# A fused decoder step on one core: 51 conditioning loads issued by ScalarE's queue instead of SyncE's

## The reference

```python
mod = (jax.nn.silu(c) @ w_ada + b_ada)[:, None, :]
sh1, sc1, gt1, sh2, sc2, gt2 = jnp.split(mod, N_MOD, axis=-1)
h = rmsnorm(x, g_pre_mix) * (1.0 + sc1) + sh1
m, k_rows, v_rows, s_new = token_mixer(h, w_in, ..., w_out, k_past, v_past, s0)
x = x + gt1 * rmsnorm(m, g_post_mix)
h = rmsnorm(x, g_pre_ffn) * (1.0 + sc2) + sh2
f = (jax.nn.silu(h @ w_ffn_gate) * (h @ w_ffn_up)) @ w_ffn_down
x = x + gt2 * rmsnorm(f, g_post_ffn)
```

## Time and profile before

| | |
|---|---|
| median of 3 runs | 1491.46 us (1487.97 to 1493.14) |
| the profiled execution | 1489.45 us, of it 1487.7 us from its first to its last instruction |
| busy, share of that span | PE 96%, PEld 85%, DVE 62%, ACT 45%, POOL 7% |
| DMA queue of SP | 319.59 MB, 63.1% of the 16 DMA engines' time |
| DMA queue of POOL | 76.10 MB, 13.5% |
| DMA queue of ACT (64 packets) | 0.07 MB, 0.0% |
| HBM traffic over the span | 265 GB/s |

### The profile page before, as it was taken

The page is one execution under the profiler, slowest core; times in us unless marked ns, Lnnn a source line. Parts: engine busy times, 40 slices in busy tenths (PEclk is TensorE's granted clock), DMA queues, the critical chain, the costliest instruction groups (busy, mean ns, idle before and its releaser), DMA issues.

```text
span 1487.7 us, 29187 instructions
## 1 busy us (share of the span) xinstructions
PE 1428.6 (96%) x11232; PEld 1270.8 (85%) x11232; DVE 922.3 (62%) x1519; ACT 665.3 (45%) x1303; POOL 105.8 (7%) x203
## 2 busy tenths in 40 slices
PE   7779999999899999999999999999999999999997
PEld 2237787887668787796999999999999999999997
DVE  2234588996778667369856766566665675446444
ACT  1023477677655554445543434334344343334333
POOL 0000311113322210000000000000000000200000
PEclk9969999999899999999999999999999999999999
DMA  9999999999999979987666666665666655855552
GB/s 368 421 341 359 388 392 406 379 345 397 392 396 336 342 258 354 404 323 278 221 181 184 178 179 179 181 185 171 183 181 174 185 173 190 233 179 181 182 177 95
DMA packets 139330, 396.82 MB, mean 267 GB/s; under 512 B 13162, under 2 KB 17681, under 8 KB 126433
## 3 DMA queue, kind: packets, MB, share of 16 engines
q1 hardware_dynamic: 117954, 319.59, 63.1%
q0 software_dynamic: 21232, 76.10, 13.5%
q10 hardware_dynamic: 64, 0.07, 0.0%
HBM read 382.28 MB, written 11.34 MB: 265 GB/s over the span
## 4 chain that ended last, share of the span: by engine, by line
PE 84%; DMA 9%; DVE 3%; ACT 2%; issue 1%; POOLq 0%; SPq 0%; POOL 0%; DVEq 0%; ACTq 0%
PE ps L1997 24%; PE ps L1998 24%; PE ps L1999 24%; PE ps L1931 4%; DMA ada_s<-in_w_ada 4%; DMA v_page<-in_cache_v 2%; PE ps L2129 2%; DMA ada_r<-in_w_ada 1%; DMA k_page<-in_cache_k 1%; PE ps L2055 1%; ACT k_page L815 1%; PE ps L1974 0%; DVE k_page L1328 0%; DVE w_lo L1277 0%; ACT w_hi L727 0%
## 5 line engine op out<-in xcount | busy, mean ns | idle before, releaser
L1997 PE MATMUL ps<-h_hi,w_hi 128*128 128x264 f32 x2304 | 666.9, 289 | 6.1 <-DVE h_lo L1265 3.6
L1998 PE MATMUL ps<-h_lo,w_hi 128*128 128x264 f32 x2304 | 658.6, 286 | 0.0
L1999 PE MATMUL ps<-h_hi,w_lo 128*128 128x264 f32 x2304 | 658.2, 286 | 0.0
L1997 PEld LDWEIGHTS ps<-h_hi,w_hi 128*128 128x128 f32 x2304 | 438.1, 190 | 49.1 <-issue 33.6
L1822 DVE TENSOR_TENSOR w_lo<-raw,w_hi 128x1024 fp32r<-128x1024 f32 x254 | 307.2, 1214 | 273.1 <-ACT w_hi L1059 271.7
L1059 ACT ACTIVATE w_hi<-raw 128x1024 fp32r<-128x1024 f32 x264 | 278.5, 1059 | 403.2 <-PE ps L1999 391.0
L1998 PEld LDWEIGHTS ps<-h_lo,w_hi 128*128 128x128 f32 x2304 | 437.4, 190 | 0.5
L1999 PEld LDWEIGHTS ps<-h_hi,w_lo 128*128 128x128 f32 x2304 | 436.3, 189 | 0.0
L1277 DVE TENSOR_TENSOR w_lo<-raw,w_hi 128x1024 fp32r<-128x1024 f32 x138 | 168.8, 1224 | 144.4 <-ACT w_hi L727 143.9
L727 ACT ACTIVATE w_hi<-raw 128x1024 fp32r<-128x1024 f32 x128 | 135.1, 1056 | 174.7 <-PE ps L1999 156.3
L1998 PE MATMUL ps<-act_lo,w_hi 128*128 (+1 forms) x704 | 200.5, 285 | 0.0
(11 more groups left out here) (363 smaller groups left out, 1217.6 us busy)
## 6 DMA issues: line engine op xcount, KB each, us to landing
ada_r<-in_w_ada SPq DMA_DIRECT2D x64, 1024.0 KB, 8.9
raw<-in_w_in SPq DMA_DIRECT2D x96, 512.0 KB, 8.4
raw<-in_w_ffn_gate SPq DMA_DIRECT2D x88, 512.0 KB, 3.7
raw<-in_w_ffn_up SPq DMA_DIRECT2D x88, 512.0 KB, 3.8
raw<-in_w_ffn_down SPq DMA_DIRECT2D x88, 512.0 KB, 4.3
ada_s<-in_w_ada SPq DMA_DIRECT2D x32, 1024.0 KB, 13.2
k_page<-in_cache_k POOLq DMA_DIRECT2D x64, 512.0 KB, 7.9
v_page<-in_cache_v POOLq DMA_DIRECT2D x38, 512.0 KB, 8.0
```

Of the source, the lines that this page charges most:

```text
L1997: mm(out, w_hi, xh, start=first, stop=False)
L1998: mm(out, w_hi, xl, start=False, stop=False)
L1999: return mm(out, w_lo, xh, start=False, stop=last)
```

## The change

The function `ada_load` gets a second copy in ACT's program, and 51 of the 64 ring rows (4 to 55, but 50) are asked for by it. The loop with its conditions is moved from SP's slot s to the end of ACT's slot st = s - 2, after the copies out of PSUM; the waits of each row move with it. Ring rows 0 to 3, 50 and 56 to 63 stay with SP, as do all units, the state loads and `x_old`.

```diff
--- before.py
+++ after.py
@@ -441,33 +441,6 @@
                     sp.wait_ge(x_moved, 32)
                     ada_load(2)
                     ada_load(3)
-                for n in range(4, 56):
-                    if n < 16 and s == A_SLOT[n - 4] + 4:
-                        ada_load(n)
-                    if 16 <= n < 18 and s == 22 + n - 16:
-                        ada_load(n)
-                    if 18 <= n < 32 and s == A_SLOT[n - 2] + 3:
-                        ada_load(n)
-                    if A_LOAD.get(n) == s:
-                        if n in (32, 33):
-
-                            sp.wait_ge(av_used, n - 1)
-                        if n == 34:
-
-                            sp.wait_ge(d_sel, 2)
-                            for i in range(2):
-                                sp.wait_ge(ktok_out[i], 32)
-                        if n == 38:
-
-                            sp.wait_ge(sb_o, H)
-                        if n in (48, 49):
-
-                            sp.wait_ge(unit_used, W_OUT)
-                        if n == 51:
-
-                            sp.wait_ge(vtok_out, 32)
-                            sp.wait_ge(rows_out, 64)
-                        ada_load(n)
                 if s == 58:
 
                     sp.wait_ge(ada_used, 32)
@@ -709,6 +682,13 @@
                 s.activation(rstd[0:64, :], ps[0:64, bank, 0:T], ACT.Ln, bias=eps_t[0:64, 0:1]).then_inc(rs_ready, 1)
                 act.wait_ge(rs_ready, 2 * (3 + x) - 1)
                 s.activation(rstd[0:64, :], rstd[0:64, :], ACT.Exp, scale=-0.5).then_inc(rs_ready, 1)
+
+            def ada_load(n):
+                q, k = divmod(2 * KC + n, KC)
+                p = ADA_PLACE[n]
+                if ADA_BEFORE[n] is not None:
+                    act.wait_ge(ada_used, ADA_BEFORE[n] + 1)
+                act.dma_start(AR[p][:, :], ada_v[:, k, PARTS[q] * 2048:PARTS[q] * 2048 + 2048]).then_inc(ada_in[ADA_SEM[n]], 16)
 
             def mod_row(q):
 
@@ -1052,6 +1032,33 @@
                     evac_frees(st // UPC)
                     for m in range(3 if st // UPC < NIN + NOUT - 1 else 0):
                         evac(st // UPC, m)
+                for n in range(4, 56):
+                    if n < 16 and st + 2 == A_SLOT[n - 4] + 4:
+                        ada_load(n)
+                    if 16 <= n < 18 and st + 2 == 22 + n - 16:
+                        ada_load(n)
+                    if 18 <= n < 32 and st + 2 == A_SLOT[n - 2] + 3:
+                        ada_load(n)
+                    if A_LOAD.get(n) == st + 2:
+                        if n in (32, 33):
+
+                            act.wait_ge(av_used, n - 1)
+                        if n == 34:
+
+                            act.wait_ge(d_sel, 2)
+                            for i in range(2):
+                                act.wait_ge(ktok_out[i], 32)
+                        if n == 38:
+
+                            act.wait_ge(sb_o, H)
+                        if n in (48, 49):
+
+                            act.wait_ge(unit_used, W_OUT)
+                        if n == 51:
+
+                            act.wait_ge(vtok_out, 32)
+                            act.wait_ge(rows_out, 64)
+                        ada_load(n)
 
             def hi_n(nb, u):
                 act.wait_ge(raw_in[u % 4], nb * 4 + (64 // 4 * (u // 4) + 16))
```

## The result

The change made the kernel slower, by a little: 1494.14 us in the median of 12 runs (1491.81 to 1496.10) against 1490.39 us of the kernel before on the same chip (12 runs, 1487.97 to 1493.14). The ratio is 1.0023, 95% interval 1.0014 to 1.0032, so +3.4 us by the ratio (2.1 to 4.8). Range and 0.3% both hold, but by luck: the time moved the other way, by losses that the sum had at nothing or as hidden. One execution of the version with row 19 back on SyncE (experiment 6) took 3193 us, the 11 others 1490.8 to 1495.2, and it is left out of the ratio there. The profiled execution took 1492.52 us, 1490.6 us of it from its first to its last instruction, 3.07 us more than the one before.

The account below looks back on a forecast made before the run. Taken as bound by TensorE, with full DMA engines costing time only where a needed transfer comes last. 1489.45 us profiled - 2.0 (stalls) + 0.5 (ScalarE) = 1488.0, median 2.0 above: 1490.0 us; range 1484.5 to 1499.5.

Parts of the forecast that it names:

- Range: Whole kernel's time forecast to lie between 1484.5 and 1499.5 us.
- 0.3%: About 4.5 us, what a measurement of this kernel can tell from no change; chance of staying within it 0.53.
- the sum: Profiled execution 1489.45 us, - 2.0 won + 0.5 lost gives 1488.0; median of the runs 2.0 above, 1490.0 us.
- Part 1: Requests at the end of ScalarE's slot come later: row 19 by 3.0 us, row 20 by 1.9, row 21 by 5.9.
- Part 2: A ring row on ScalarE's queue lands in 6.9 us: 4.6 transfer, 2.3 other; bounds 4.8 and 15.8.
- Part 3: TensorE's stalls at ring rows 19 and 20, 3.46 us: 2.0 won, 1.5 given back; bounds 0.5 and 3.5.
- Part 4: ScalarE's 14 requests in 200 to 345 us, 6.6 us, mostly hidden: 0.5 us lost at the GLA tree.
- Part 5: SP's weights: no gain; K pages: 0.9 us per ring row, hidden by five pages in flight, otherwise 2.7 us.
- A: Ring rows land as slowly as before, only the later requests remain: 7.9 us slower, 1499.4 us; chance 0.12.
- B: TensorE waits for ScalarE: 6.6 us of requests and 2.7 of pages surface, + 7.3, 1498.8 us; chance 0.12.
- D: ScalarE lags so far that requests fall behind the units as before: time as now, 1491.5 us; chance 0.05.
- C: All 3.46 us stay won and V page waits halve: - 3.5 - 5.0, 1483 us; chance 0.18.

Follow-up runs that it names:

- experiment 6: Kernel after the change with ring row 19 alone asked for by SyncE in its old slot: 1492.79 us, ratio 1.0011 to the kernel before.
- experiment 7: Kernel before, all rows by SyncE, but ring rows 19 and 20 asked for ahead of the weight unit in slots 30 and 32: 1492.67 us, 1.0020.
- experiment 2: Kernel before, with ScalarE also issuing 512-byte DMAs to DRAM in the change's 51 places behind the same waits: 1490.39 us, 1.0001.
- the control of experiment 5: Kernel before with group 3's PSUM copies ahead of slot 31's w_hi: three copies 1490.74 us, 0.9996; all four 1490.65 us, 1.0005.

## Why the prediction was wrong

**Part 1 (later requests)** held for two rows of three. Counted from the start of unit 31, which comes 1.46 us earlier in this execution, row 19 was asked for 2.3 us later (3.0 forecast: 218.53 against 217.71), row 21 6.9 us later (5.9), and row 20 0.3 us sooner (1.9 later). I had read each time off the end of the engine's work in front of the request. But ScalarE's queue issues a request while the engine still works off what stands ahead of it: row 20 was asked for at 223.46, before the high part in front of it began at 224.90. The quicker landing covered all three.

**Part 2 (landing)** held in its mechanism: packets go one for one (59, 62 and 68 in 222 to 224 us), and the 128 packets of row 19 ran from 222.06 to 226.57, of row 21 from 242.19 to 246.58, 4.5 and 4.4 us against the 4.6 of the sum. What is not transfer was too small: 2.3 us forecast, 4.6 and 4.1 found, of it 3.5 and 3.0 between the request and the first packet. So rows 19 and 20 took 9.1 and 8.6 us and not 6.9.

**Part 3 (stalls)** was right about the rows: both stalls for them are gone. I expected 2.0 us of 3.46 to stay won; the stretch from unit 33 to 34 shows 1.65 won, that of row 20. The other 1.87 us, before unit 32, turned into 5.02. I did see that a row may overtake a weight unit, but put it at row 20 and a later unit (0 to 2.3 us given back at row 21); it was row 19 and unit 34, whose high part ScalarE makes in the very slot at whose end it has a group to copy.

**Part 4 (ScalarE's time)**: 0.5 us lost was forecast, none found (1.0001 with all 51 requests, which could hide 1.3 us); a request took 0.33 us, not 0.47.

**Part 5 (what the others lose) is the step that failed.** "SP's queue holds only weights, issued when the low part is done, as now; no gain" took that queue's loss as nothing: while row 19 was served it passed 68 packets in 2 us where it had passed 144, and unit 34 landed 3.8 us later. For K pages it put 0.9 us on each of 14 rows, "hidden by five pages in flight; if that cover fails, three more waits of 0.9, 2.7 us". Those 0.9 us are what a third queue adds to a row's eight turns, and they leave out when the turns fall. In the kernel before, row 19's packets started at 224.3, 2.1 us before K page 15 had landed; now they start at 222.1, 6.0 us before it does, and POOL's queue passes 62 packets in 2 us and not 149. Page 15 took 2.5 us longer and pages 16 to 18 2.4 to 3.2 us. The cover did fail, and the profile had said so: VectorE already waited for K pages in this stretch, and a transfer that is waited for has no cover left. VectorE's waits for K pages now:

```profile
DVE k_page L1335 <- DMA k_page<-in_cache_k: 5.9, 4, 3.6
```

**Not in the sum at all:** the granted clock. Behind one idle of 5.0 us, unit 32 took 2.2 us longer at 1.2 GHz, where 3.46 us in three pieces had cost nothing. Without it these units would have come out 1.4 us above the kernel before.

The rivals: A (own queue helps nothing) and B (ScalarE's requests) are refuted, D too. For C, the V page waits moved from 10.1 to 11.5 us, the wrong way for it and less than the 3 us that I had named. The rule of the Trainium skill that I set beside A ("DMA: Bandwidth & Descriptors", section "Issuing engines are not separate DMA queues": one saves only the time to issue) speaks of the sum of the work, and for that the trace agrees, 6.17 MB against 6.11 in 15 us; the landings (rows 19 to 21 in 8.4 to 9.1 us, down from 13.9 to 15.8) show that it says nothing of whose transfer comes first, and here that decided.

**What stays open.** Why 3.0 to 3.5 us pass between a row's request on ScalarE's queue and its first packet; which of rows 18 and 21 makes the loss when 19 and 20 stay with SyncE; and what decides whether the granted clock falls behind an idle. No version that I ran beats the kernel before.

## What to carry to other kernels

While the DMA engines are full, a transfer that comes sooner makes another come later. Before giving a load its own queue, list what else is under way in those microseconds with the time at which each is used, and ask which has the least slack; here row 20 had 11 us in hand where it landed, while K page 15 and unit 34 were waited for already. And when one stall is traced to a late transfer, moving the work that queues behind it only hands the stall to the next work in line.

## What the runs showed of the hardware

Queues that have work divide full DMA engines by packets, nearly one for one, and not by bytes: 59 packets of 8 KB, 62 of 4 KB and 68 of 2 KB on three queues in the same 2 us, 0.48, 0.23 and 0.13 MB. So a load in large packets takes most of the engines' time from the others while it is served (58.9%), and the same holds when it stands on a queue with other loads (68.2% in experiment 7). ScalarE's queue issued a DMA request up to 1.4 us before the instruction ahead of it in the program had begun. After an idle TensorE may be granted half its clock for a time, and the length of the idle alone doesn't tell: 5.02 us of idling was followed by 0.50 in 235 to 240 us and 3.19 us by a mean of 0.66, and in experiment 2 idles of 2.35 and 0.61 us lay in a stretch (230 to 235 us) with a mean of 0.80; but in the control of experiment 5 idles of 2.74 and 2.22 us, ten microseconds apart, by 1.00.
